# The forget-gated heads' q, k and v by seven products for eight, as the dilated heads' are: one decoder layer on one core

## The reference

```python
x = x + 0.5 * swiglu(rmsnorm(x, ffn1_norm), ...)            # D_FF = 5632
proj = rmsnorm(x, mix_norm) @ w_in                          # (256, 2048) @ (2048, 6*1024 + 8 + 2*2048)
q_d, k_d, v_d, q_f, k_f, v_f, f_logit, g_d, g_f = split(proj)
y_dil = dilated_attention(rope(q_d) * scale, rope(k_d), v_d)     # 8 heads of 128
log_f = log_sigmoid(f_logit + b_forget)
y_fox = forgetting_attention(q_f * scale, k_f, v_f, log_f)       # logits += sum of log f between key and query
x = x + (sigmoid(g_d + b) * (y_dil @ w_proj_dil) + sigmoid(g_f + b) * (y_fox @ w_proj_fox)) @ w_out
x = x + 0.5 * swiglu(rmsnorm(x, ffn2_norm), ...)
```

## Time and profile before

| | |
|---|---|
| median of 3 runs | 2050.8 us (2050.64 to 2051.0) |
| the profiled execution | 2050.62 us, of which the span from first to last instruction is 2048.8 us |
| TensorE busy in the span | 2032.5 us (99%), 9222 matmuls |
| VectorE busy | 1823.2 us (89%) |
| ScalarE busy | 1256.5 us (61%) |
| granted TensorE clock | 0.999 of 2.4 GHz |

### The profile page before, as it was taken

One profiled execution on the slowest core, in us unless ns is written; L12 is line 12 of the kernel. 1 busy time (PEld: TensorE's weight loads), 2 busy tenths in 40 slices (PEclk: granted clock), 3 DMA queues, 4 the chain that ended last, 5 costly groups with the idle time before them and its releaser, 6 DMA issues.

```text
span 2048.8 us, 26355 instructions
## 1 busy us (share of the span) xinstructions
PE 2032.5 (99%) x9222; PEld 1681.5 (82%) x9222; DVE 1823.2 (89%) x1861; ACT 1256.5 (61%) x1462; POOL 87.6 (4%) x80
## 2 busy tenths in 40 slices
PE   9999999999999999999999999999999999999998
PEld 7788888888888887888888888888888888888886
DVE  7999999999999788755589999889999999999997
ACT  7666666666666556654565555566666666666664
POOL 0000000000000000000000000000000000000000
PEclk9999999999999999999999999999999999999999
DMA  8578777787877454645446575655878777887773
GB/s 287 205 219 253 239 232 245 226 238 227 245 246 241 150 185 169 209 162 182 153 152 207 193 236 175 218 185 188 259 208 257 245 230 211 260 230 235 247 228 131
DMA packets 222143, 441.03 MB, mean 215 GB/s; under 512 B 7649, under 2 KB 7825, under 8 KB 221937
## 3 DMA queue, kind: packets, MB, share of 16 engines
q1 hardware_dynamic: 202112, 401.64, 56.5%
q0 software_dynamic: 19744, 38.28, 11.2%
q10 hardware_dynamic: 208, 0.08, 0.0%
HBM read 400.13 MB, written 2.10 MB: 196 GB/s over the span
## 4 chain that ended last, share of the span: by engine, by line
PE 94%; DVE 3%; ACT 1%; issue 1%; DMA 0%; SPq 0%; ACTq 0%; DVEq 0%
PE ps L736 17%; PE ps L738 16%; PE ps L737 16%; PE ps L749 11%; PE ps L751 11%; PE ps L750 11%; PE ps L947 2%; PE ps L946 2%; PE ps L948 2%; PE ps L801 1%; PE ps L998 1%; PE ps L996 1%; PE ps L997 1%; PE ps L782 0%; ACT w_hi L1293 0%
## 5 line engine op out<-in xcount | busy, mean ns | idle before, releaser
L1756 DVE TENSOR_TENSOR w_lo<-raw,w_hi 128x1024 fp32r<-128x1024 f32 x280 | 338.3, 1221 | 7.1 <-ACT w_hi L1306 5.0
L1306 ACT ACTIVATE w_hi<-raw 128x1024 fp32r<-128x1024 f32 x280 | 290.9, 1053 | 71.8 <-PE ps L738 52.8
L1306 ACT ACTIVATE w_hi<-sums 128x1024 fp32r<-128x1024 f32 x160 | 169.9, 1063 | 209.5 <-PE ps L738 72.6
L1717 DVE TENSOR_TENSOR w_lo<-raw,w_hi 128x1024 fp32r<-128x1024 f32 x116 | 141.2, 1224 | 96.0 <-ACT w_hi L1293 95.3
L1756 DVE TENSOR_TENSOR w_lo<-sums,w_hi 128x1024 fp32r<-128x1024 f32 x160 | 195.6, 1224 | 34.5 <-ACT w_hi L1306 31.9
L736 PE MATMUL ps<-w_hi,xT_hi 128*128 128x512 f32 x552 | 221.0, 400 | 0.4 <-DVE xT_lo L1792 0.4
L738 PE MATMUL ps<-w_hi,xT_lo 128*128 128x512 f32 x552 | 215.6, 390 | 0.0
L737 PE MATMUL ps<-w_lo,xT_hi 128*128 128x512 f32 x552 | 215.1, 390 | 0.0
L736 PE MATMUL ps<-w_hi,hT_hi 128*128 128x512 f32 x536 | 208.8, 390 | 0.0
L738 PE MATMUL ps<-w_hi,hT_lo 128*128 128x512 f32 x536 | 208.5, 389 | 0.0
L737 PE MATMUL ps<-w_lo,hT_hi 128*128 128x512 f32 x536 | 208.5, 389 | 0.0
(11 more groups left out here) (352 smaller groups left out, 4770.3 us busy)
## 6 DMA issues: line engine op xcount, KB each, us to landing
raw<-in_ffn_w_up SPq DMA_DIRECT2D x88, 1024.0 KB, 5.7
raw<-in_ffn_w_down SPq DMA_DIRECT2D x88, 1024.0 KB, 5.3
raw<-in_ffn_w_gate SPq DMA_DIRECT2D x87, 1024.0 KB, 5.4
raw<-in_w_in SPq DMA_DIRECT2D x80, 1024.0 KB, 5.1
xres<-gate_buf POOLq DMA_DIRECT2D x72, 512.0 KB, 5.5
raw<-in_w_out SPq DMA_DIRECT2D x16, 1024.0 KB, 5.3
raw<-in_w_proj_dil SPq DMA_DIRECT2D x8, 1024.0 KB, 5.9
raw<-in_w_proj_fox SPq DMA_DIRECT2D x8, 1024.0 KB, 5.6
```

Of the source, the lines that this page charges most:

```text
L1306: nc.scalar.activation(slot_hi(place, offset), src, ACT.Copy).then_inc(hi_ready, 1)
L1717: nc.vector.tensor_tensor(slot_lo(place, offset), raw_half(place, offset), slot_hi(place, offset).bitcast(F32), ALU.subtract).then_inc(lo_ ...
L1756: nc.vector.tensor_tensor(slot_lo(place, offset), step_source(r)[0], slot_hi(place, offset).bitcast(F32), ALU.subtract).then_inc(lo_ready, 1)
```

## The change

- The six chunks of the forget-gated heads become pairs 3, 4 and 5 of the same `dil_pair` (q, k, v halves side by side), each of the 19-slab form: one group by seven, the rest direct. Their weight sums lie in `v_sb`, their partial sums in `fox_partial`; the token sums `third_hi`/`third_lo` move to where they last until pair 5.
- The slots of dilated attention are put behind direct slabs of these pairs (`DIL_SLOTS` by pair and slab), with head outputs in bank M1 and turned tiles in bank M6, since banks 4 to 7 now belong to the products. A slot behind the products (slabs 13 and 16) waits for `dil_combined` of the third sum of its pair.
- In the pairs' loop on VectorE the up chunk's last sum stands ahead of the split of the slab four further on; the token sums of group 2 move from pair 1 to pair 0.
- In the first chunk of the first SwiGLU the first four slabs run in the order high-high, high-low, low-high (`first_wide`), with one round and one split exchanged before them; squares of x move behind later slabs (`FIRST_SQUARES`).

```diff
-D_SLABS, D_LOADS = (19, 19, 22), 8
+D_SLABS, D_LOADS = (19, 19, 22, 19, 19, 19), 8
+F_PAIR = 3
...
-D_SEVEN, D_GATE, D_UP = zip(_QK, _QK, _V)
+D_SEVEN, D_GATE, D_UP = zip(_QK, _QK, _V, _QK, _QK, _QK)
...
+    FIRST_SQUARES = {4: (0, 1), 6: (2,), 7: (3,)}
...
-    SUM_FORGET = 6
+    SUM_FORGET = 5
-    DIL_SLOTS = {4 + 4 * s: s for s in range(HEADS + 2)}
+    FOX_Q_TURNS, FOX_K_TURNS = (15, 17), (1, 2)
+    DIL_SLOTS = {(3, 3): 0, (3, 13): 1, (3, 16): 2, (4, 0): 3, (4, 3): 4, (4, 13): 5, (4, 16): 6,
+                 (5, 0): 7, (5, 3): 8, (5, 13): 9}
+    SLOTS_AHEAD = {3: 0, 4: 4, 5: 8}
+    DIL_HEAD_OUT, FOX_QK_T = D_M1, D_M6
...
+            def first_wide(o, banks):
+                ...
+                pe.wait_ge(hi_ready, place.slab(o + 1))
+                for t in range(TT):
+                    pe.wait_ge(xt_hi, n + t + 1)
+                    for j in range(2):
+                        nc.tensor.matmul(ps[:, banks + t, :], xT_hi[:, 2 * o + j, tokens(t)], hi_w[:, j],
+                                         start=o == 0 and j == 0, stop=False)
+                pe.wait_ge(lo_ready, place.slab(o + 1))
...
+            def transpose_fox(c, part, t):
+                pe.wait_ge(evac, (2 * c + part + 1) * TT)
+                pe.wait_ge(qk_out, fox_count(c, part, t))
...
                     if s == 0 and o == 4:
                         pe.wait_ge(dil_combined, c * D_COMBINED)
+                        if c == F_PAIR:
+                            pe.wait_ge(f_rows_lo, 1)
...
+                    if (c, r) in DIL_SLOTS:
+                        if r > D_SEVEN[c][-1][0]:
+                            pe.wait_ge(dil_combined, c * D_COMBINED + 3)
+                        attend(DIL_SLOTS[c, r], 0)
...
-            place = mix_place(FOX)
-            for c in range(6):
-                half, part = divmod(c, 3)
-                banks = A if c % 2 == 0 else B
-                for o in range(WIDE):
-                    wide(place, c * WIDE, banks, o)
...
             for e in range(D_TOTAL):
-                split_dil(e + MIX_RING)
                 c, r, _ = dil_slab(e)
+                if r == D_SLABS[c] - 1:
+                    dve.wait_ge(slab_done, place.slab(D_SLABS[c]))
+                    nc.vector.tensor_tensor(gate_buf[:, 1], ps[:, D_UP1:D_UP1 + TT], gate_buf[:, 1],
+                                            ALU.add).then_inc(dil_combined, 1)
+                split_dil(e + MIX_RING)
...
+                if c == 0 and r == last + 8:
+                    sum_tokens_of(2, 2)
-                if c == 1 and r == 3:
-                    sum_tokens_of(2, 2)
...
+                if c == F_PAIR and r == SUM_FORGET + 2:
+                    nc.vector.tensor_tensor(f_rows[F_LO:F_ROWS, :], ps[F_LO:F_ROWS, HEAD_OUT, 0:SEQ], ...)
```

More of the change, by code:

```diff
@@ L970, in transpose_dil @@
                     done = nc.tensor.transpose(ps[:, QK_T, k * P:(k + 1) * P],
+                                               source[:, k * P:(k + 1) * P], ident)
+                done.then_inc(qk_raw, 1)
+            def transpose_fox(c, part, t):
+                pe.wait_ge(evac, (2 * c + part + 1) * TT)
+                pe.wait_ge(qk_out, fox_count(c, part, t))
+                source = gate_buf[:, part, 1 - t if part else t]
+                for k in range(CT):
+                    done = nc.tensor.transpose(ps[:, FOX_QK_T, k * P:(k + 1) * P],
                                                source[:, k * P:(k + 1) * P], ident)
@@ new lines, in _ @@
+            for e in range(D_TOTAL):
+                round_dil(e + MIX_RING)
+                c, r, _ = dil_slab(e)
+                place = dil_place(c)
+                last = D_SEVEN[c][-1][0]
+                if c == 0 and r == 1:
+                    round_tokens_of(3, 1)
+                if c == 0 and r == last + 9:
+                    round_tokens_of(2, 2)
+                if c > 0 and r == 0:
+                    evacuate_dil(c - 1, 1)
+                if r in DIL_TURNS[c]:
+                    n = (c - 1) * 2 * TT + DIL_TURNS[c].index(r)
+                    copy_qk(n // TT % 2, slice((c - 1) * CT, c * CT), n % TT, n, QK_T)
+                if c == F_PAIR and r == 1:
+                    act.wait_ge(f_abs_ready, 1)
+                    nc.scalar.activation(f_soft[:, :, :], f_abs[:, :, :], ACT.Exp).then_inc(f_exp, 1)
+                    act.wait_ge(f_exp, 1)
+                    nc.scalar.activation(f_soft[:, :, :], f_soft[:, :, :], ACT.Ln, bias=1.0)\
+                      .then_inc(f_soft_ready, 1)
+                if c == F_PAIR and r == SUM_FORGET + 1:
+                    act.wait_ge(f_summed, 1)
+                    nc.scalar.activation(f_rows[:, :], ps[0:F_ROWS, HEAD_OUT, 0:SEQ],
+                                         ACT.Copy).then_inc(f_rows_hi, 1)
+                if fox_turn(c, r) is not None:
+                    pair, part, t = fox_turn(c, r)
+                    at = HEADS + (pair - F_PAIR) * CT
+                    copy_qk(part, slice(at, at + CT), t, fox_count(pair, part, t), FOX_QK_T)
+                if (c, r) in DIL_SLOTS:
+                    attend(DIL_SLOTS[c, r], 0)
+                if r == last + 3:
+                    act.wait_ge(slab_done, place.slab(last + 2))
+                    parts = partial if c < F_PAIR else fox_partial
+                    nc.scalar.activation(parts[:, PART_M1], ps[:, D_M1], ACT.Copy).then_inc(dil_m1_copied, 1)
+                if r == last + PAIR_SLABS + 1:
+                    evacuate_dil(c, 0)
```

312 lines of the change are left out of this document (143 added, 169 removed).

## The result

The changed kernel takes 2054.4 us (median of 20 runs, 2052.67 to 2056.23), the kernel before 2050.9 (2050.64 to 2051.19): a ratio of 1.0016, 95% interval 1.0009 to 1.0022. It is 3.5 us or 0.17% slower, inside the bound of 0.2%; the forecast was 0.8 us slower. Its runs spread over 3.6 us where the kernel before spreads over 0.6. The profiled execution took 2055.9 us with a span of 2054.1.

What follows compares the result with a forecast made beforehand. TensorE, busy for 99% of the span, was taken as the bound. Terms of -4.1 - 2.8 - 1.3 + 5.9 + 3.1 = +0.8 us gave a median of 2051.6 us, range 2048.0 to 2055.2.

Steps and rivals of the forecast that it cites:

- Matmuls: In the forget-gated chunks made pairs, 576 matmuls become 558; 18 fewer at 0.227 us each, a gain of 4.1 us.
- Dilated pairs: Two turning waits for the up chunk's sum (2.1 us) and one wait in pair 1's products (0.7) go: 2.8 us gained.
- Start: Waits of the first matmul and two first-step products go; gain 1.3 us, bounds 0 and 1.4.
- Third sum: The slot behind slab 13 waits for VectorE's third sum: 2.1 us in pairs 4 and 5, 1.7 in pair 3; +5.9.
- Forget rows: Slab 10 of pair 3 waits for the forget rows from VectorE: +3.1 us, bounds 0.4 and 4.
- every added wait of TensorE is paid in full: Premise for the whole kernel: TensorE is busy 99% of the span, so each added wait costs its own length.
- Products of pairs 4 and 5: Slower rival: these products are late as pair 3's, through the slot behind slab 3; up to 4 us, 2055.6; chance 0.17.
- the work costed at nothing: Nine more slabs to round and split, twelve weight sums, nine combining operations, and VectorE's slot work in pairs 4 and 5: 0 us.
- Slot waits: Faster rival: waits for the third sum are not felt; 5.9 us fall away, 2045.7, or 2042.6 with pair 3's; chance 0.10.
- the start gives nothing back: Rival at the kernel's start: no gain there, 2052.9 us; counted inside the no-change case, which had 0.73.

Runs made afterwards that it cites:

- start_reorder: The kernel before with the change's start and the dilated pairs' reordering together, without the forget-gated pairs; 2045.70 us, ratio 0.9976.
- reorder_only: The kernel before with only the dilated pairs' reordering: up chunk's last sum ahead of the split, token sums of group 2 in pair 0; 2047.89 us, ratio 0.9986.
- start_only: The kernel before with only the change's start: first four slabs high-high first, squares later, rounding and splitting order of the first slabs; 2048.77 us, ratio 0.9992.
- filled: The changed kernel with unused identity transposes ahead of the forget rows' wait and each slab 13 wait for the third sum; 2051.57 us, ratio 1.0004.
- forget_bank: The changed kernel with the forget rows summed in bank 6 instead of bank 7 and waited for at slab 13; 2053.97 us, ratio 1.0016.
- sum10: The changed kernel with VectorE making the third sum right behind the second instead of two slabs later; 2050.70 us, ratio 1.0000.
- slot14: The changed kernel with the attention slots of pairs 3, 4 and 5 behind slab 14 instead of 13; 2051.36 us, ratio 1.0004.
- slot14_turns: On top of slot14, the turns of the forget-gated q behind slabs 17 and 18 instead of 15 and 17; 2048.95 us, ratio 0.9993.

## Why the prediction was nearly right, and where it failed

By medians the changed kernel is 3.5 us above the one before, and 8.7 above start_reorder. Step by step:

- *Matmuls, -4.1.* 9204 are there. Not measured by itself.
- *Dilated pairs, forecast -2.8, measured -2.9* (reorder_only). In the changed kernel both turns and pair 1's products go without a wait.
- *Start, forecast -1.3, measured -2.0* (start_only). The upper bound of 1.4 was wrong, since this term was added up from brackets, unlike the one of the dilated pairs. A bracket counts idle time from the end of the operation ahead, and that end lies 0.16 to 0.25 us later than the place where a next start could have stood. The starts in the trace of before:

```profile
9.81 0.66 PE L1107 MATMUL ps<-tab 128*128 128x128 f32 x4
...
68.87 0.39 PE L751 MATMUL ps<-w_hi,xT_lo 128*128 128x512 f32 x1
...
72.24 0.39 PE L751 MATMUL ps<-w_hi,pair_lo 128*128 128x512 f32 x1
```

The two later waits are 69.61 - 68.87 - 0.23 = 0.51 us and 73.10 - 72.24 - 0.23 = 0.63, not 0.35 and 0.47. The first matmul starts 1.04 us behind the four transposes ahead of it, and 0.41 in the changed kernel and start_only, so 0.63 and not 0.38. Together with the 0.1 us of each slower start this is the 2.0.

- *Third sum, forecast +5.9, measured +5.1 in the changed kernel and +6.1 in filled.* Slots of pairs 4 and 5: 2.02 each, forecast 2.1. Pair 3: 1.04, forecast 1.7; TensorE had come later by the slow stretch ahead, and without that stretch it is 2.04. The two splits stand ahead of the sum as counted:

```profile
921.15 0.69 DVE L2199 TENSOR_TENSOR fox_partial<-ps,fox_partial 128x512 f32<-128x512 f32 x1
...
922.48 2.35 DVE L2130 TENSOR_TENSOR w_lo<-raw,w_hi 128x1024 fp32r<-128x1024 f32 x2
...
924.75 1.22 DVE L2210 TENSOR_TENSOR gate_buf<-ps,fox_partial 128x1024 f32<-128x1024 f32 x1
```

- *Forget rows, forecast +3.1, measured +2.8:* 2.44 at slab 10, and about 0.4 at slab 9, which I had not told apart. The rows are there at 863.10 + 0.43 = 863.53, which is 26.4 us after pair 3's start at 837.08, as counted; TensorE comes 0.8 us later than counted, which is the difference:

```profile
863.10 0.43 DVE L2248 TENSOR_TENSOR f_rows<-ps,f_rows 64x256 fp32r<-64x256 f32 x1
```

- *Not foreseen, +0.5 (+0.1 in filled):* the turn behind slab 15 of pair 3 waits for ScalarE's evacuation. It looked small, and was the next link once the third sum was moved.
- *Not foreseen, the clock: +2.8 net* by the medians of changed kernel and filled; three slow stretches of together 5.0 us in the profiled execution. This is the step that failed. The prediction took a wait of TensorE at its own length ("every added wait of TensorE is paid in full"), and behind waits of about 2 us it can be paid nearly twice. In pair 3 1.0 us of the loss is covered, because the next wait ends when VectorE is done (1.04 us instead of 2.04).

Since the 2.8 us of the clock are net of what they cover, the waits are added as filled has them: -4.1 - 2.9 - 2.0 + 6.1 + 2.8 + 0.1 + 2.8 = +2.8. Some 0.7 us of the 3.5 are left, for which no run was made. The traces show where such time stands: from pair 3's start to the first mask matmul (`tri_b`) of the attention that follows, filled takes 157.5 us (837.08 to 994.59) and start_reorder 151.7 (836.88 to 988.62). With the 4.1 us of matmuls that is 9.9 us more, of which the waits are 9.0; the other 0.9 is in slower first steps behind waits and in the slots' own matmuls.

Filled, which is the changed kernel without the fall of the clock, took 2051.57, and the forecast was 2051.6. That it agrees to 0.1 us is luck in part: the start gave 0.7 us more than forecast, the dilated pairs 0.1 more, and the forget rows cost 0.3 less; against this stand 0.2 us more at the slots, 0.1 at the turn and the 0.9 of small times. The mechanism of the waits was right to 0.3 us in each term but the start's.

The rivals. Products of pairs 4 and 5 were not late: no bracket stands there, so the work costed at nothing cost nothing that shows. Slot waits were felt. That the start gives nothing back is refuted by start_only. The forecast range was right for the wrong reason on its high side: what filled it was the clock.

Why no simple repair gave what I expected of it: all edited versions took away the wait that they aimed at (forget_bank all but 0.65 us of it), and save for the earlier forget gate about half or more of the expected gain was lost at the next door (third sum, evacuation, normalised rows), since behind the products one chain runs from VectorE's third sum and gate sum over the maxima and exponentials to the evacuation and the turn. What is shown is this order in sum10's timelines. That putting the evacuation ahead of the exponentials, or the slots at distances of three slabs from slab 14 on, would free the chain is only argued: it was not tried.

## What to carry to other kernels

When a block with much TensorE work per operand (direct chunks) is replaced by one with less work and more sums, the saved matmuls are sure and small, and every place where TensorE meets the helpers' chain has to be counted; here 18 matmuls saved 4.1 us and the meeting places cost over 11, clock included. None of the versions with the forget-gated pairs reached the 2045.7 us of the one without them; the best of them by median took 2048.5. A wait on the engine that bounds the kernel is priced at its length plus the possible half-clock stretch behind it, and a spread of the runs that grows from 0.6 to 3.6 us is a sign of it. If the wait cannot be avoided, transposes that fill the idle time ahead of it give back the second part (2.8 us here). Add waits from start to start less a step, not from brackets. Before a wait is removed, ask who of the chain is late next: removing one gave at most 3.7 us of an expected 8.

## What the runs showed of the hardware

In the profiled executions of the changed kernel and its eight edited versions without fillings, TensorE waited 19 times between 1.76 and 2.78 us in pairs 3 to 5. Around the end of 11 of them the granted clock fell from its level of 2.4 to that of 1.2 GHz, between 0.7 us before work resumed and 1.2 us after, and stayed there for some 3.4 us each time, at a cost of 1.7 us (rows of the granted clock in steps of 0.1 us); behind the other 8 it stayed at 1.00. Behind the shorter ones, of up to 1.66 us, it never fell. The same wait of 2.27 us at slab 10 was followed by a fall in the changed kernel, slot14 and sum10, and not in slot14_turns. It isn't a matter of the single execution alone: all eleven runs of sum10 have a granted clock of 0.998, as with one slow stretch, while eight of the eleven of slot14_turns have 0.999, as with none. What decides between the two is open.

The Trainium skill, page "TensorE: Matmul & The Clock Gate", section "HAM oscillation — how this bites in real kernels", describes a kernel whose TensorE falls to half clock behind each wait for data, and prices it as the slow time multiplied by a half. The rows agree with that price: the slow stretch of pair 3 lasts some 3.4 us, by the page's price an estimated 1.7 us, and the window gives 1.7.
